# The recurrent layer's preparation rewritten: k-tile hand-over of blends and projections, padded tokens, packed key roots, decays beside the first projection

## The chip, the cores and the metric

One core of one Trainium2 chip. The metric is the device time of one execution in microseconds (us). In the profile PE is TensorE (matmul) and PEld its weight load, DVE is VectorE, ACT ScalarE, POOL GpSimd and SP SyncE.

## The reference

Two blocks follow one another: first two hybrid layers (sparse attention, gated linear attention, pooling, a convolved feed-forward), then four layers with a gating mixer, a recurrent mixer, a latent attention and again a gating mixer. Only the features of the recurrent mixer are touched. It runs over 768 tokens: 256 of context and 512 of the sequence, which are two separate sequences. In fp32, with 16 heads of 64:

```
h    = rms_norm(x) * (1 + scale) + shift
xx   = 0.5 * (previous token + next token) - h      # zero beyond either end of each sequence
xs_c = h + xx * mu_c                                # six blends, c = 0..5
r, k, v, z = xs_0 @ W_0, xs_1 @ W_1, xs_2 @ W_2, xs_3 @ W_3      # 1024 x 1024 each
w_n  = w0_n + tanh(xs_4 @ L1_n) @ L2_n              # decays, n = two directions, rank 64
a_n  = sigmoid(a0_n + (xs_5 @ A1_n) @ A2_n)
kk   = (k * k_k) / sqrt(sum over the head of (k * k_k)^2 + 1e-12)
k_n  = k * (1 + (a_n - 1) * k_a)
bonus sums: sum over the head of r * r_k * (k_0 + k_1), times v
```

The scan that follows reads r, kk, k_n, kk * a_n, v and the decays of both directions; the output reads z and the bonus.

## The kernel before

Activations lie with the 1024 channels on partitions, as 8 tiles (k when they are read, m when they are written), and the tokens in the free dimension, in two segments of 256 and 512 (`segs`). Weights come in slabs of 2048 columns (1 MB) into a ring of 4 slots; SyncE issues the loads in a fixed order, and each waits until the slab four places earlier is used up. The order here is rw_l1 0, rw_l1 1, rw_l2, then four slabs each of rw_in for r, k, v and z; a slab holds two tiles m. PSUM has 8 banks, each taken in turn from a ring by `take` and freed by the instruction that reads it last. Each engine has its own program, written out by hand and in order; semaphores are the only links. Four functions write the stage: `features_pe_`, `features_act`, `features_dve`, `features_pool`.

The stage goes as follows. Squares for the norm are summed beside the layer before. `roots_dve`, `roots_act` and `spread_pe` (L478) make and spread the inverse roots, `normed_dve` (L490) scales all 16 pieces, `modulated_act` (L1504) shifts them. When all are there, VectorE makes xx in seven instructions (L1901 to L1905), then a blend of eight instructions into the one buffer `xs` (`lerp_dve`, L1889). TensorE multiplies blend 4 by the first low-rank weights, in four products (two directions, two segments, 64 columns wide); then VectorE writes blend 5 into the same buffer, and so on in the order 4, 5, 0, 1, 2, 3. TensorE waits for the last tile of a blend, and VectorE for the last product of the blend before:

```
    lerp_dve(pl, e, 4)
    e.wait_ge(*S_.lora_made.at(4, 1, 256))
    lerp_dve(pl, e, 5)
```

After the low rank come 24 products for the decays (L330), whose sigmoids (L1801) go to memory through two stages, then r: 8 tiles of 16 products (L518), copied by VectorE (L1921) and stored.

For k, the work of a tile lies beside the next tile's projection, behind its first segment: in `derive` TensorE makes four products of the rates a (L1734) and sums the squares of the scaled keys over the head with the table blk64 (L360), ScalarE copies k (L1838), takes the sigmoids (L1815), one square (L378) and the square root (L382), VectorE scales the keys (L1934), squares one segment (L396), adds the epsilon (L401), takes the reciprocal over all 768 columns on all partitions (L404, 1.75 us for 256 columns and 3.35 for 512), normalizes (L1936), mixes (L1941) and multiplies (L1944). GpSimd multiplies the two k_n (L1998) and issues five stores a tile. The keys, the rates and k_n have one buffer each, so ScalarE waits for the stores of one tile before it writes the rates of the next. The sums for the bonus (L1744) come two tiles later. v has transposes (L336) behind its second segment, which wait for ScalarE's copy of the same tile (L1857). z has only the projection (L1868).

Of the kernel before, what the change touches and what calls it, by code (L numbers as in the profile page):

```python
# [9 lines left out]
ALU = mybir.AluOpType  # L10
# [184 lines left out]
DMA_SIGNALS = ("const", "cols", "x_in", "pos", "sgu_w", "sgu_b", "res", "a2", "lw0", "lw1", "r_out", "kk_out",  # L195
# [271 lines left out]
def spread_pe(pl, e, key, segs):  # L467

    S_ = pl.S
    e.wait_ge(*S_.inverse_roots.at(key))  # L470
    for seg in segs:
        o, n = quarters(segs, seg)
        at = ("rs", key, seg[0])
        ps = take(pl, at)
# [1185 lines left out]

def lay_features(pl):
    A, b = Arena(pl), Place()
    b.segs = list(NSEG)
    b.h, b.xx, b.xs = A(8, N), A(8, N), A(8, N)
    b.hk = lambda k, s: b.h[:, k, s[0]:s[0] + s[1]]
    b.tw, b.ta, b.a2 = A(2, N), A(2, N), A(2048)
    b.sq = [A(512), A(512)]
    at = A.at
    b.stage = [A(1024) for _ in range(2)]
    A = Arena(pl, at)  # L1670
    b.kr, b.kb, b.an, b.kd = A(2, N), A(N), A(2, N), A(2, N)
    b.rs, b.omk, b.cfs = A(N), A(8), A(2, N)
    A = Arena(pl, at)
    b.vv, b.bo, b.vt = A(2, N), A(2, N), A(2, N)
    A = Arena(pl, at)
    b.zz = A(2, N)
    b.x = lambda k, s: b.xs[:, k, s[0]:s[0] + s[1]]
    return b


LERPS = (4, 5, 0, 1, 2, 3)
# [11 lines left out]

def features_pe_(pl, e):
    S_, b = pl.S, pl.feat
    segs = b.segs
    spread_pe(pl, e, ("mod", 1), BOTH)
    for c in (4, 5):
        key = ("rw_l1", c - 4)
        w = slab(pl, key, 1024, 8)  # L1700
        e.wait_ge(*landed(pl, key))
        e.wait_ge(*S_.lerped.at(c))
        for n in range(2):
            for seg in segs:
                at = ("lora", c, n, seg[0])
                ps = take(pl, at)[0:64, 0:seg[1]]
                e.wait_ge(*free(pl, at))
                product(e, ps, [(w[:, k, 64 * n:64 * n + 64], b.x(k, seg)) for k in range(8)]).then_inc(
                    *S_.lora_made.next((c, n, seg[0]), slab=key if n == 1 and seg is segs[-1] else None))
    key = "rw_l2"  # L1710
    l2 = pl.W[:, pl.slot_of[key], 0:2048]
    e.wait_ge(*landed(pl, key))
    e.wait_ge(*S_.lora_act.at(4))
    e.wait_ge(*S_.shifted.at("ones"))
    for n in range(2):
        for a in range(6):
            for hf in range(2):
                at, o = ("decay", n, a, hf), 1024 * n + 512 * hf
                ps = take(pl, at)
                e.wait_ge(*free(pl, at))  # L1720
                product(e, ps[:, :], [(b.tw[0:65, n, P * a:P * a + P], l2[0:65, o:o + 512])]).then_inc(
                    *S_.lora_made.next((n, a, hf), slab=key if (n, a, hf) == (1, 5, 1) else None))
    features_pe(pl, e, "rw_r", [("rw_in", 0, c) for c in range(4)], 8, 256, b.x, segs, [S_.lerped.at(0)])

    def derive(m):
        for n in range(2):
            for sg in segs:
                at, o = ("iclr", m, n, sg[0]), 1024 * n + P * m
                ps = take(pl, at)[:, 0:sg[1]]
                if m == 0 and n == 0:  # L1730
                    e.wait_ge(*S_.a2.at("in"))
                    e.wait_ge(*S_.lora_act.at(5))
                e.wait_ge(*free(pl, at))
                e.matmul(ps, b.a2[0:64, o:o + P], b.ta[0:64, n, sg[0]:sg[0] + sg[1]], start=True,  # L1734
                         stop=True).then_inc(*S_.iclr_out.next((m, n, sg[0])))
        rms_pe(pl, e, ("kk", m), [rows_of(b.kb)], segs, b.sq, table(pl, "blk64"))

    def bonus(m):
        for sg in segs:
            at = ("bonus", m, sg[0])  # L1740
            ps = take(pl, at)[:, 0:sg[1]]
            e.wait_ge(*S_.bonus_in.at(m))
            e.wait_ge(*free(pl, at))
            e.matmul(ps, table(pl, "blk64"), b.cfs[:, m % 2, sg[0]:sg[0] + sg[1]], start=True, stop=True).then_inc(  # L1744
                *S_.bonus_sums.next((m, sg[0])))

    def behind_k(m, seg):
        if seg[0] == 0 and m > 1:
            bonus(m - 2)
        if seg[0] == 0 and m > 0:  # L1750
            derive(m - 1)

    features_pe(pl, e, "rw_k", [("rw_in", 1, c) for c in range(4)], 8, 256, b.x, segs, [S_.lerped.at(1)],
                beside=behind_k)
    derive(7)
    bonus(6)
    bonus(7)

    def behind_v(m, seg):
        if seg[0] == 0:  # L1760
            return
        y = b.vv[:, m % 2, :]
        e.wait_ge(*S_.act_projected.at("rw_v", m, segs[-1][0]))
        for sg in segs:
            at = ("v_t", m, sg[0])
            ps = take(pl, at)
            e.wait_ge(*free(pl, at))
            for a in range(sg[1] // P):
                t = turned(pl, e, ps[:, P * a:P * a + P], y[:, sg[0] + P * a:sg[0] + P * a + P])
            t.then_inc(*S_.value_turned.next((m, sg[0])))  # L1770

    features_pe(pl, e, "rw_v", [("rw_in", 2, c) for c in range(4)], 8, 256, b.x, segs, [S_.lerped.at(2)],
                beside=behind_v)
    features_pe(pl, e, "rw_z", [("rw_in", 3, c) for c in range(4)], 8, 256, b.x, segs, [S_.lerped.at(3)])
# [3 lines left out]
def features_act(pl, e):  # L1778
    S_, b = pl.S, pl.feat
    segs = b.segs  # L1780
    modulated_act(pl, e, 1, b.hk, BOTH, lambda k, seg: [S_.residual_added.at(("sgu_o", 0), k, seg[0])])
    e.dma_start(b.a2[0:64, :], pl.ins["rw_l2"][1][0:64, :]).then_inc(*S_.a2.next("in"))
    for c, dst in ((4, b.tw), (5, b.ta)):
        for n in range(2):
            for seg in segs:
                at = ("lora", c, n, seg[0])
                e.wait_ge(*S_.lora_made.at(c, n, seg[0]))
                e.activation(dst[0:64, n, seg[0]:seg[0] + seg[1]], bank(pl, at)[0:64, 0:seg[1]],
                             ACT.Tanh if c == 4 else ACT.Copy).then_inc(
                    *S_.lora_act.next(c, frees=at) if n == 1 and seg is segs[-1] else S_.lora_act.next(frees=at))  # L1790
    u = 0
    for n in range(2):
        for a in range(6):
            for hf in range(2):
                at = ("decay", n, a, hf)
                e.wait_ge(*S_.lora_made.at(n, a, hf))
                if u == 0 and hf == 0:
                    e.wait_ge(*S_.modulated.at(1))
                if u >= 2:
                    e.wait_ge(*(S_.lw1 if u % 2 else S_.lw0).at(u - 2))  # L1800
# [1836 lines left out]
```

## Time and profile before

| | us |
|---|---|
| runs before (3) | 5655.90, 5662.35, 5680.89; median 5662.35 |
| profiled execution, its own time | 5677.09 |
| its span | 5675.3 |
| TensorE busy | 5066.3 (89%) |
| VectorE, ScalarE, GpSimd busy | 1594.8, 1054.0, 416.5 |
| mean granted clock of TensorE | 0.92 of full speed |
| the changed stage, 2647.0 to 3294.3 | 647.3 |

The times below are from the start of the span. A matmul of fp32 data is two records in the trace, each with a weight load. A row of the timeline merges like instructions that follow one another and names the form of the first; in brackets stands how long the engine was idle before it and what released it. The granted clock is a share of 2.4 GHz.

### The profile page before, as it was taken

To read this page: it belongs to the slowest core of one execution; us is meant where nothing else is said; L and a number is where in the kernel's file an instruction comes from. 1 tells how busy PE (TensorE), PEld (TensorE's weight loads), DVE (VectorE), ACT (ScalarE), POOL (GpSimd) and SP (SyncE) were. 2 spreads that over 40 slices of the span, in tenths; PEclk is the share of its full clock that TensorE was granted. 3 is DMA by queue.
4 is the path that set the end of the run, shared out by engine and by line. 5 is a ranking of instruction groups with operands and counts; after the bars stand their busy time and mean duration, and the time that the engine had idled before them with its cause. 6 is when DMAs were issued, how large, how long until landed. Compare 5 with 4: busy or idle time off the path is not lost. (4 is left out here: it accounts for less than half of the span.)

```text
span 5675.3 us, 62648 instructions
## 1 busy us (share of the span) xinstructions
PE 5066.3 (89%) x27214; PEld 2803.4 (49%) x27214; DVE 1594.8 (28%) x2792; ACT 1054.0 (19%) x2044; POOL 416.5 (7%) x331
## 2 busy tenths in 40 slices
PE   7879999978999999997976968887589999989999
PEld 3444444444444446654433557777344455554444
DVE  1261110144111101002144145655520244430000
ACT  1121000022100111101122023333111233321210
POOL 1110000010000000000022011111000010100000
PEclk9869999977999999998987988888789999989999
DMA  3222222122121111111322222111111100001221
GB/s 114 89 105 74 82 68 83 60 104 104 67 82 66 61 59 52 52 45 56 108 72 85 80 79 63 50 49 45 77 56 51 41 23 25 29 30 67 82 74 59
DMA packets 91567, 378.27 MB, mean 67 GB/s; under 512 B 7904, under 2 KB 33504, under 8 KB 61792
## 3 DMA queue, kind: packets, MB, share of 16 engines
q1 hardware_dynamic: 74688, 318.00, 16.3%
q0 software_dynamic: 9808, 37.75, 2.0%
q10 hardware_dynamic: 6800, 18.52, 0.9%
q8 instruction: 217, 3.56, 0.3%
q14 instruction: 54, 0.44, 0.0%
HBM read 334.40 MB, written 39.85 MB: 66 GB/s over the span
## 5 line engine op out<-in xcount | busy, mean ns | idle before, releaser
L518 PE MATMUL ps<-A,W 128*128 128x512 f32 (+1 forms) x6496 | 2546.9, 553 | 48.6 <-DVE A L1889 21.3
L518 PEld LDWEIGHTS ps<-A,W 128*128 128x128 f32 x6496 | 1248.1, 193 | 1307.5 <-issue 1213.6
L330 PE MATMUL ps<-A 64*64 64x64 f32 (+3 forms) x8416 | 522.0, 243 | 89.8 <-ACT A L3180 23.2
L330 PEld LDWEIGHTS ps<-A 64*64 64x64 f32 (+2 forms) x8416 | 479.9, 153 | 203.5 <-issue 124.8
L330 PE MATMUL ps<-A,W 128*128 128x512 f32 (+5 forms) x1728 | 454.7, 431 | 48.9 <-issue 39.1
L539 PE MATMUL ps<-W,A 128*128 128x512 f32 (+1 forms) x896 | 365.6, 571 | 1.8 <-ACT A L1504 1.8
L330 PEld LDWEIGHTS ps<-A,W 128*128 128x128 f32 (+2 forms) x1728 | 226.0, 165 | 260.1 <-issue 242.0
L539 PEld LDWEIGHTS ps<-W,A 128*128 128x128 f32 x896 | 173.1, 194 | 192.6 <-issue 186.9
L432 ACT ACTIVATE A<-R 128x512 f32<-128x512 f32 (+1 forms) x96 | 52.6, 574 | 805.2 <-DVE R L1514 376.5
L1634 DVE SCALAR_TENSOR_TENSOR A<-ps,V,A 128x512 f32<-128x512 f32 (+1 forms) x48 | 31.0, 661 | 486.9 <-PE ps L330 486.3
L1514 DVE SCALAR_TENSOR_TENSOR R<-ps,MOD,R 128x512 f32<-128x512 f32 (+1 forms) x48 | 31.8, 662 | 461.8 <-PE ps L518 449.7
L360 PE MATMUL ps<-A,C 128*128 128x256 f32 (+1 forms) x64 | 48.7, 861 | 126.2 <-ACT A L378 63.5
L330 PE MATMUL ps<-W,A 64*64 64x64 f32 (+4 forms) x1904 | 157.7, 263 | 3.5 <-ACT A L2389 2.8
L1650 POOL TENSOR_TENSOR A<-A 128x1536 f32<-128x1536 f32 (+1 forms) x16 | 46.4, 2901 | 1533.5 <-ACT A L1607 1533.5
L336 PE MATMUL ps<-C,A 128*128 128x128 f32 x608 | 105.3, 300 | 49.6 <-DVE A L1184 44.0
L330 PEld LDWEIGHTS ps<-W,A 64*64 64x64 f32 (+2 forms) x1904 | 128.0, 160 | 37.5 <-issue 31.9
L2159 PE MATMUL ps<-C,A 128*128 128x256 f32 x192 | 69.2, 524 | 82.4 <-DVE A L2596 66.6
L3171 ACT ACTIVATE A<-ps,A 128x256 f32<-128x256 f32 (+1 forms) x128 | 84.8, 668 | 302.7 <-DVE A L3292 302.7
L336 PEld LDWEIGHTS ps<-C,A 128*128 128x128 f32 x608 | 72.4, 149 | 135.0 <-DVE A L1184 62.2
L1448 DVE TENSOR_TENSOR A<-A,ps 128x512 f32<-128x512 f32 x44 | 30.3, 689 | 334.1 <-PE ps L518 334.1
L1607 ACT ACTIVATE A<-ps 128x256 f32<-128x256 f32 (+1 forms) x96 | 50.3, 526 | 369.9 <-PE ps L518 369.7
L3290 DVE TENSOR_REDUCE A<-ps 128x1 f32<-128x256 f32 (+1 forms) x128 | 71.4, 558 | 142.6 <-PE ps L2955 142.1
(328 smaller groups left out, 4268.4 us busy)
## 6 DMA issues: line engine op xcount, KB each, us to landing
W<-in_ada SPq DMA_DIRECT2D x48, 1024.0 KB, 5.2
W<-in_w_up SPq DMA_DIRECT2D x44, 1024.0 KB, 4.8
W<-in_w_down SPq DMA_DIRECT2D x32, 704.0 KB, 4.0
W<-in_w_in SPq DMA_DIRECT2D x18, 1024.0 KB, 4.9
W<-in_sgu_v SPq DMA_DIRECT2D x16, 1024.0 KB, 4.9
W<-in_sgu_u SPq DMA_DIRECT2D x16, 1024.0 KB, 4.9
W<-in_sgu_z SPq DMA_DIRECT2D x16, 1024.0 KB, 4.9
W<-in_sgu_o SPq DMA_DIRECT2D x16, 1024.0 KB, 4.8
```

What stands on the lines that cost most here:

```text
L330: r = e.matmul(out, a, b, start=start and i == 0, stop=stop and i == len(pairs) - 1, skip_group_check=loose)
L336: return e.transpose(out, in_, table(pl, "ident")[0:k, 0:k])
L360: e.matmul(ps, ones[0:k, :], y, start=i == 0, stop=i == len(xs) - 1).then_inc(*S.squares_summed.next((key, n), (key, "of", seg[0])) if i = ...
L432: e.activation(pl.sq[k % 2][:, cols], pl.R[:, k, cols], ACT.Square).then_inc(*S_.act_squares.next((key, k, seg[0])))
L518: t = e.matmul(ps, w[:, k, c:c + mc], x(k, seg), start=k == 0, stop=k == kt - 1)
L539: mm = e.matmul(ps, x(k0 + k, tile), w[:, k, :], start=k0 + k == 0, stop=k0 + k == kt - 1)
L1514: e.scalar_tensor_tensor(out=r, in0=bank(pl, at)[:, 0:seg[1]], scalar=modulation(pl, i, 2, m, seg), in1=r, op0=ALU.mult, op1=ALU.add).then ...
L1607: e.activation(dst[:, m, o:o + seg[1]], bank(pl, at)[:, 0:seg[1]], func).then_inc(*signal.next((i, g), frees=at) if m == 1 and seg is segs ...
L1650: e.tensor_tensor(b.uu, b.uu, b.zz, ALU.mult).then_inc(*S_.sgu_gated.next((i, g)))
L2159: t = e.matmul(ps[:, 256 * i:256 * i + 256], b.LW[:, P * (2 * j + i):P * (2 * j + i) + P], table(pl, f"tri{n}"), start=True, stop=True)
L3171: e.activation(b.pr[:, z, lo:hi], bank(pl, at)[:, 0:hi - lo], ACT.Exp, bias=m[:, 2:3], scale=b.rq[:, p % 2, 2 * i + j:2 * i + j + 1], accu ...
L3290: e.tensor_reduce(m[:, part:part + 1], bank(pl, at)[:, 0:w], AX, ALU.max).then_inc(*made.next())
```

## The change

The four functions are written anew; the rest of the kernel calls them as before.

- Tokens are padded. h, xx and xs have 771 columns, with a zero column at either end and one between the segments, so that the neighbours of all 769 inner columns are one add.
- The first blends go by k tile. VectorE scales tile k (both segments), then adds the neighbours of tile k-1 and finishes the blends 4 and 5 of it; blend 5 has a buffer of its own, `x2`. ScalarE has shifted the tile and written h * (1 - mu) for both; a blend is then that plus 0.5 * mu times the sum of neighbours. TensorE multiplies each k tile as it comes, into six banks. The second low-rank product has both directions in one product of 128 columns (the weights a2 lie on 128 rows).
- Blend 0 is made in the same way while ScalarE sees each k tile of blend 4 used. The others (1, 2, 3) are made from xx as before, but each k tile is written as soon as the last tile m = 7 of the projection before has read it; that tile and the first, m = 0, run with k outside and both segments inside.
- The decays are no longer a part of their own: four products stand behind each of r's tiles 0 to 5.
- Banks: projections take 6, 7, 0, 1, the rest 2, 3, 4, 5.
- Key roots are packed: the squares of 4 groups of 192 tokens are summed into 4 x 32 partitions (`sums`), so root and reciprocal work on 192 columns, and `spread` brings them back to all rows, by halves. VectorE's one instruction then scales by k_k and the root from PSUM; ScalarE's square takes k_k as its scale over all 768 columns.
- Keys and rates have two buffers with stores of their own; the k_n keep one. Rates stand behind the tile's own second segment, sums and spread one tile later. Transposes of v come one tile later. The bonus product is written in place.

The core of the diff:

```diff
+def wave_pe(pl, e, c, name, ready, beside):
+    S_, b = pl.S, pl.feat
+    for m in range(8):
+        key = ("rw_in", c, m // 2)
...
+        e.wait_ge(*landed(pl, key))
+        if m in (0, 7):
...
+            for k in range(8):
+                if m == 0:
+                    e.wait_ge(*ready(k))
+                for y, s in zip(ps, b.segs):
+                    t = e.matmul(y, w[:, k, :], b.x(k, s), start=k == 0, stop=k == 7)
...
 def features_pe_(pl, e):
+    for k in range(8):
+        e.wait_ge(*S_.lerped.at(4, k))
+        for n in range(2):
+            for i, s in enumerate(segs):
+                t = e.matmul(ps[2 * n + i][0:64, 0:s[1]], w[0][:, k, 64 * n:64 * n + 64], b.x(k, s), start=k == 0,
+                             stop=k == 7)
...
+        e.wait_ge(*S_.lerped.at(5, k))
+        for i, s in enumerate(segs):
+            t = e.matmul(ps[4 + i][:, 0:s[1]], w[1][:, k, :], b.y(k, s), start=k == 0, stop=k == 7)
...
+                e.matmul(ps[:, :], b.tw[0:65, n, P * a:P * a + P], l2[0:65, o:o + 512], start=True, stop=True).then_inc(
+                    *S_.lora_made.next(at, slab=key if (u, hf) == (11, 1) else None))
+
+    wave_pe(pl, e, 0, "rw_r", lambda k: S_.lerped.at(0, k), decay)
...
+    def sums(m):
...
+        for c in range(4):
+            t = e.matmul(ps[32 * c:32 * c + 32, 0:192], table(pl, "blk64", 48, 80),
+                         pl.sq[m % 2][:, 192 * c:192 * c + 192], start=True, stop=True)
...
+    def spread(m):
+        for j in range(2):
...
+            e.wait_ge(*S_.inverse_roots.at("kk", m))
+            e.wait_ge(*free(pl, at))
+            for c in range(2):
+                for i, half in enumerate(HALF):
...
+                    t = e.matmul(ps[half, 192 * c:192 * c + 192], row, pl.root[:, 0:192], start=True, stop=True)
...
+    def behind_k(m, lo):
+        if not lo:
+            if m:
+                sums(m - 1)
+            if m > 1:
+                bonus(m - 2)
             return
+        rates(m)
+        if m:
+            spread(m - 1)
...
 def features_dve(pl, e):
+    for k in range(9):
...
+            e.tensor_tensor(b.xx[:, j, INNER], b.h[:, j, 0:N + 1], b.h[:, j, 2:N + 3], ALU.add).then_inc(
+                *S_.shifted.next())
+            e.wait_ge(*S_.shifted.last())
+            part(b.xs, 4, j)
+            part(b.x2, 5, j)
...
+    for m in range(9):
+        if m:
+            root(m - 1)
+            coefficients(m - 1)
+            if m == 7:
+                for k in range(8):
+                    lerp(2, k, "rw_k")
+            normed(m - 1)
+        if m < 8:
+            mixed(m)
```

## Rows read from the trace of the kernel before

**Rows 1.** Windows view, the changed stage: us; each engine's busy time (instructions); clock; DMA.
```profile
2647.00:3294.30 647.30, 494.35 (x1409) 268.48 (x1408) 212.90 (x221) 110.23 (x188) 102.90 (x100) 0.85 0.26 85
```

**Rows 2.** Waits view of TensorE, 2640 to 3330: us in total, times, longest.
```profile
PE ps L360 <- ACT A L378: 50.9, 8, 9.4
```

**Rows 3.** Timeline of all engines, head: start us, us, engine, line, operation [idle before].
```profile
2650.18 1.35 DVE L464 RECIPROCAL A<-A 128x192 f32<-128x192 f32 x1 [0.80 <-ACT A L454]
...
2651.59 3.78 PE L478 MATMUL ps<-A,C 128*128 128x64 f32 x16 [2.64 <-DVE A L464]
...
2653.70 8.49 DVE L490 SCALAR_TENSOR_TENSOR A<-R,MOD,ps 128x256 f32<-128x256 f32 x16 [2.16 <-PE ps L478]
...
2654.27 8.67 ACT L1504 ACTIVATE A<-A,MOD 128x256 f32<-128x256 f32 x16 [4.12 <-DVE A L490]
...
2679.20 7.53 DVE L1889 SCALAR_TENSOR_TENSOR A<-A,V 128x768 f32<-128x768 f32 x8
```

**Rows 4.** Timeline of TensorE, low rank to the first k tiles.
```profile
2686.83 23.26 PE L330 MATMUL ps<-A,W 128*64 128x256 f32 x64 [31.45 <-issue]
...
2717.75 23.16 PE L330 MATMUL ps<-A,W 128*64 128x256 f32 x64 [7.67 <-issue]
...
2740.84 20.87 PE L330 MATMUL ps<-W,A 65*128 65x512 f32 x48
...
2761.54 82.72 PE L518 MATMUL ps<-A,W 128*128 128x256 f32 x256
...
2852.55 15.53 PE L518 MATMUL ps<-A,W 128*128 128x256 f32 x48 [8.29 <-DVE A L1889]
```

**Rows 5.** Timeline of TensorE, one k tile of the steady part.
```profile
2889.96 1.56 PE L1744 MATMUL ps<-A,C 128*128 128x256 f32 x4 [1.84 <-DVE A L1951]
...
2891.45 2.84 PE L1734 MATMUL ps<-A 64*128 64x256 f32 x8
...
2903.25 2.05 PE L360 MATMUL ps<-A,C 128*128 128x512 f32 x2 [8.32 <-ACT A L378]
...
2905.09 11.34 PE L518 MATMUL ps<-A,W 128*128 128x512 f32 x32
...
2919.24 1.77 PE L1744 MATMUL ps<-A,C 128*128 128x256 f32 x4 [2.81 <-DVE A L1951]
```

**Rows 6.** Timeline of TensorE, the starts of v and z.
```profile
3102.29 13.48 PE L518 MATMUL ps<-A,W 128*128 128x256 f32 x32 [4.50 <-DVE A L1889]
...
3116.46 0.88 PE L336 MATMUL ps<-C,A 128*128 128x128 f32 x6 [0.69 <-ACT A L1857]
...
3209.00 85.28 PE L518 MATMUL ps<-A,W 128*128 128x256 f32 x256 [8.48 <-DVE A L1889]
```

**Rows 7.** Timeline of ScalarE, in the same k tile.
```profile
2897.57 1.28 ACT L1815 ACT_TABLE_LOAD   x1 [5.41 <-DMA f_ka<-A]
...
2898.86 1.99 ACT L1815 ACTIVATE A<-ps,V 128x256 f32<-128x256 f32 x4
...
2902.49 0.61 ACT L378 ACTIVATE A<-A 128x512 f32<-128x512 f32 x1
```

**Rows 8.** Timeline of VectorE and GpSimd, in the k tile before.
```profile
2883.16 2.17 DVE L1941 TENSOR_SCALAR A<-A,V 128x768 f32<-128x768 f32 x1
...
2882.46 2.45 POOL L1998 TENSOR_TENSOR A<-A 128x768 f32<-128x768 f32 x1 [36.34 <-DVE A L1941]
```

**Rows 9.** Timeline of TensorE, a later stage (64-column products of two halves).
```profile
4312.31 10.57 PE L2910 MATMUL ps<-A,W 128*64 128x256 f32 x64
```

**Rows 10.** Windows view: after a long wait; one k tile.
```profile
2686.80:2691.50 4.70, 4.67 (x11) 2.59 (x12) 0.00 (x0) 0.00 (x0) 0.00 (x0) 0.50 0.01 3
...
2889.96:2919.24 29.28, 18.14 (x48) 9.43 (x49) 14.78 (x13) 8.09 (x13) 9.00 (x8) 0.83 0.24 68
```

**Rows 11.** Tile view, loads of rw_in (x16) and of rw_out (x4, together).
```profile
DMA to landing us min/median/max: 4.7/5.2/6.8
...
DMA to landing us min/median/max: 5.6/10.4/15.0
```

More of the change, by code:

```diff
@@ L1710, in features_pe_ @@
[L1710 to L1736, printed above, removed]
+    segs, side = b.segs, "2345"
@@ L1738, in bonus @@
     def bonus(m):
-        for sg in segs:
-            at = ("bonus", m, sg[0])
-            ps = take(pl, at)[:, 0:sg[1]]
+        for s in segs:
+            at = ("bonus", m, s[0])
+            ps = take(pl, at, side)[:, 0:s[1]]
             e.wait_ge(*S_.bonus_in.at(m))
             e.wait_ge(*free(pl, at))
[L1744 to L1760, printed above, removed]
-            return
+            e.matmul(ps, table(pl, "blk64"), b.cfs[:, m % 2, s[0]:s[0] + s[1]], start=True, stop=True).then_inc(
+                *S_.bonus_sums.next((m, s[0])))
+    def behind_k(m, lo):
[4 more added lines that the diff above has]
+                bonus(m - 2)
+            return
+        rates(m)
+        if m:
+            spread(m - 1)
@@ L1791, in features_act @@
-    u = 0
-    for n in range(2):
[L1793 to L1800, printed above, removed]
-                e.activation(b.stage[u % 2][:, 512 * hf:512 * hf + 512], bank(pl, at)[:, :], ACT.Sigmoid).then_inc(
-                    *S_.decay_act.next((u, hf), frees=at))
-            u += 1
@@ new lines, in features_act, with root @@
+    for u in range(12):
+        if u >= 2:
+            e.wait_ge(*(S_.lw1 if u % 2 else S_.lw0).at(u - 2))
+        for hf in range(2):
+            at = ("decay", u, hf)
+            e.wait_ge(*S_.lora_made.at(at))
+            e.activation(b.stage[u % 2][:, 512 * hf:512 * hf + 512], bank(pl, at)[:, :], ACT.Sigmoid).then_inc(
+                *S_.decay_act.next((u, hf), frees=at))
+    def root(m):
+        x = pl.root[:, 0:192]
+        e.wait_ge(*S_.mean_squares.at("kk", m))
+        e.activation(x, x, ACT.Sqrt).then_inc(*S_.roots.next(("kk", m)))
@@ L1844, in features_act @@
-    derive(7)
-    bonus(6)
-    bonus(7)
+            if m >= 2 and s is segs[0]:
+                e.wait_ge(*S_.value_turned.at(m - 2, segs[1][0]))
+                e.wait_ge(*S_.bonus_made.at(m - 2))
+            e.activation(b.vv[:, m % 2, s[0]:s[0] + s[1]], bank(pl, at)[:, 0:s[1]], ACT.Copy).then_inc(
+                *S_.act_projected.next(at, frees=at))
+            if s is segs[0] and m == 0:
+                root(7)
+            if s is segs[0] and m < 2:
+                bonus(6 + m)
@@ L1908, in features_dve @@
+    for k in range(8):
+        part(b.xs, 0, k)
     e.memset(b.tw[64:65, :, :], 0.0).then_inc(*S_.shifted.next())
```

492 lines of the change are left out of this document (299 added, 193 removed).

## The prediction

> **What bounds the kernel now.** The profiled execution took 5677.1 us (span 5675.3), 14.7 above the median of the runs, 5662.35. The change touches one stage. The windows view cuts it out, from the last matmul of the gating layer (2647.0) to the last z matmul (3294.3) [rows 1]: 647.3 us with TensorE busy for 494.4 at a mean granted clock of 0.85. No other engine is busy for more than a third, so the stage is bound by TensorE and by what TensorE waits for. The waits view names the largest cause: eight waits of matmuls for the squares of the key norms [rows 2]. The timelines then give six stretches, whose bounds are starts of matmuls:
> - head, 2647.0 to 2686.8: 39.8 us, TensorE nearly idle while VectorE and ScalarE make h, its shift and the first blend [rows 3, 4]
> - low rank, to 2740.8: 54.0, two projections of 23.2 with a blend's wait of 7.7 between them [rows 4]
> - decays and r, to 2844.3: 20.7 and 82.7, dense [rows 4]
> - k, to 3102.3: 258.0, with 8.3 of blend wait ahead [rows 4], then a period of 29.3 a tile; 2889.96 to 2919.24 is one, and the others have this form [rows 5]
> - v, to 3209.0: 106.7, 11.9 a tile and a blend wait of 8.5 [rows 6]
> - z, to 3294.3: 85.3 [rows 6].
>
> They sum to 647.3.
>
> **The change, part by part.** *Head.* The spread roots are complete at 2651.6 + 3.8 = 2655.4; VectorE now waits for both segments, 1.7 later than before. Its 16 normed pieces take 8.5, so 1.06 a k tile, and a blend over 768 columns 0.94 (8 in 7.53) [rows 3]. Per k tile it now does 1.06, an add and two blends: 1.06 + 3 x 0.95 + 0.15 for dependent starts (my estimate) = 4.1. ScalarE has 1.1 of shifting [rows 3] and two scalings of some 0.9 (0.61 for 512 columns [rows 7]) = 2.9, hidden behind 4.1; if VectorE were free, 2.9 would be the pace. POOL's three memsets and the constants that VectorE makes lie under the squares and roots; without that cover they would cost under 1. The first blend is ready after two norms, an add and a blend: 2655.5 + 4.2 = 2659.7. Head 12.7, saved 27.1.
>
> *Low rank.* Projection 4 has the same matmuls; projection 5 has both directions in one 128-column product, half as many. At full rate 768 columns over 8 k take 10.3 (82.7 for eight tiles [rows 4]); so 20.6 + 10.3 = 31, 3.9 a k. VectorE brings a k each 4.1, so it sets the pace and TensorE, 95% busy, ends behind it: 2655.5 + 8 x (1.06 + 2.95) = 2687.6, last products 2689.4. The first 4.7 us after a long wait run at 0.50, the low level of 1.2 GHz [rows 10]; the 2.3 lost are caught up in the slack. 29.7 against 54.0, saved 24.3.
>
> *Decays beside r.* The same products, 20.7 + 82.7 = 103.4 [rows 4]. The blend for r costs VectorE 7.5 from 2687.6 and TensorE takes 1.3 a k for the first tile, so it is not late; the row of ones and the tanh end near 2698, ahead of the first decay at 2699.6. But the weight ring has four slots, and the fourth r slab goes into that of the second-stage decay weights. Until now that was free before r began; now the last decay, at the end of tile 5, frees it and tile 6 needs it at once. SP stands at that load, and the first three k slabs are issued right behind it. Bounds: such a load landed in 4.7 at best; of four issued together the first landed in 5.6, the last in 15.0 [rows 11]. I take 5.6 + 0.3 for the signal, since ours is the first of four. After the 8.3 wait at 2852.55 the next 48 matmul records took 15.5, where dense ones take 13.8 (1.33 tiles of 10.3) [rows 4]: 1.7 more. Stall 7.6. 111.0 against 103.5, lost 7.5. The sigmoids' waits for stores were off the path and stay so.
>
> *k.* Off the path go the roots over 768 columns on all rows, the extra scaling pass, the single buffers that held ScalarE for a store [rows 7], and the blend's wait at the start (r's last tile hands k tiles back one by one, each blend 0.95, each use 1.3). TensorE per tile: rates 2.84, bonus 1.6, projection 10.3 [rows 4, 5]; packed sums, four column groups of 192, some 0.5; two spreads, together 768 columns in pairs of halves. Halves run together: line 2910 has 12288 columns in 64 records, twice the 6144 of a full-width tile, in 10.6 [rows 9], the time of one tile. So the spreads are 1.3; were they apart, 2.6. One wait stays: the spreads need banks that the rates' sigmoids free. After the tile's last product ScalarE has copy 0.6, square 0.85, table load and the first sigmoids [rows 7]: 0.1 + 0.6 + 0.05 + 0.85 + 1.29 + 0.45 = 3.35, and 3.85 for the second. TensorE has done its 2.84 and waits 0.5 to 1. Tile period: 4.9 (rates, wait, spreads) + 10.3 + 0.5 + 1.6 + 0.2 = 17.5. The others must fit: ScalarE 7.8 (copies 2.0, square 0.85, loads 2.6, root 0.4, sigmoids 2.0); VectorE 9 to 12 (root 0.4 + 1.35 for 192 columns [rows 3], coefficients 2.0, norms 1.1, products 1.9, mixes 1.3 to 4); POOL two multiplies of 2.45 [rows 8] and five stores, 9.2. All fit, and each link of the chain (sums at 8.5 after the tile, root by 12, spread at 17.5 + 3.4) has 5 us to spare. First tile 10.3, second 13.7, five of 17.5, last 4.9 + 10.3: 126.7. Late next: VectorE's blends for v stand behind root 6, whose sums TensorE makes only after tile 7. Root at 4.0, coefficients 6.0, first blend 7.0; TensorE's spread of tile 6 waits for sigmoids and is over at 8.0. So v starts at 134.7. Against 258.0, saved 123.3.
>
> The Trainium skill (ScalarE: Activation LUTs, What ACT_TABLE_LOAD costs) gives a switch of sets 1283 ns plus a drain of about 1380. The trace shows only the first: the load at 2897.57 is followed by its activation at 2898.86 [rows 7], so the measurement decides. By the page the wait for the banks would be 1.4 longer in each of eight tiles, an estimate of 11 us more.
>
> *v.* Eight tiles 82.6; turns 0.9 each [rows 6], now a tile later and so without their 0.7 wait, 6.2; sums, bonuses and spread of tile 7, 4.9; 2.0 of wait for root 7 (VectorE does the eight blends first); 2.1 for z's first blend, behind turn 6: 97.8, saved 8.9. *z.* 82.6 and one turn: 83.5, saved 1.8; its last store is where it was, so the scan starts as before. Four gaps of 1 to 3 us remain. After one of 2.8 the group in [rows 5] came late and the next was slow, and 3 to 5 us at half rate lose about 2; I add 3 in all (0 to 6).
>
> Sum: 27.1 + 24.3 - 7.5 + 123.3 + 8.9 + 1.8 - 3 = 174.9. The profiled execution would take 5502; against the median, 5487.
>
> Later stages are not edited, but they enter the shared ring of banks at another turn: price 0, bounded by 3 either way, since each such bank has whole tiles of slack.
>
> **Rivals.** (1) *The k loop is paced by another engine.* For: a scaling of VectorE took 2.17 while POOL multiplied [rows 8], and all work in a tighter ring of banks. Against: busy times of 8 to 12 under 17.5. A period of 22 gives 6 x 4.5 = 27 more: 5514. (2) *The clock stays low in the low-rank stretch.* For: a k tile with TensorE 62% busy had a clock of 0.83 [rows 10]. Against: 95% busy here. At half rate 31 us of products are 62: 32 more, 5519. (3) *A switch of tables costs twice its row*, 1.3 in each of eight tiles: 5497. (4) *Slower: stores hold the k loop.* For: before, ScalarE waited 5.4 for a store in each tile [rows 7]. If the single kd buffers hold the next rates, nothing overlaps: TensorE 14.6, square, root, spread, norms, mixes, multiplies and coefficients 18, stores 4.2, and a landing of 6.8 to 15.0 [rows 11] give 43.6 to 51.8 a tile. It loses from 17.5 + 175/7 = 42.5 on and gives 5670 to 5727. Against: only VectorE's mix waits for that store, and it landed half a tile earlier. (5) *The fourth slab lands with the last of its burst*, 15.0: 10 more, 5497.
>
> **How the numbers follow.** Own sum 0.60, rival 1 0.14, rival 2 0.06, rival 3 0.05, rival 4 0.02, rival 5 0.10, and 0.03 for a part that gains nothing (the head and low rank, or half of k: about 5545). Own bounds: landing -1, gaps -3, later stages -3, pace -2 and the scatter of runs 8 make 5470; upward alike, 5505. The range takes in rivals 1, 2, 3 and 5: 5470 to 5524. A measurement of this kernel tells about 0.5% (28 us) from no change; only rival 4 is not beyond it: faster 0.97, same 0.01, slower 0.02.
>
> **What would show it.** Right: the first low-rank matmul some 13 us after the gating layer's last; its products in groups each 4.1; a gap of 5 to 7 between r's tiles 5 and 6, ended by a landing; k starts without a gap, 17.5 a tile; gaps of about 2 before v's second tile and before z; the stage 472 us, clock above 0.95. Wrong: a period over 20 with VectorE or POOL named, a low-rank stretch at 0.5, a slab gap over 9, or a scan that starts late.

## The result and the profile after

The changed kernel takes 5491.86 us (median of 4 runs, 5480.95 to 5501.22) against 5666.45 (4 runs, 5655.9 to 5680.89): a ratio of 0.969, 95% interval 0.9659 to 0.972, 174.6 us less. Forecast were 5487 and a range of 5470 to 5524. In a later comparison of five rounds the ratio was 0.9699 (0.9671 to 0.9727).

The head of the page of the changed kernel; the profiled execution took 5480.95 us:

```profile
span 5479.2 us, 62884 instructions
...
PE 4986.2 (91%) x27342; PEld 2765.4 (50%) x27342; DVE 1544.5 (28%) x2779; ACT 1070.9 (20%) x2058; POOL 406.8 (7%) x334
```

The windows view over the changed stage, which answers to [rows 1], whole and by the six stretches of the prediction (us; busy time of TensorE, its weight loads, VectorE, ScalarE, GpSimd, with instructions; granted clock; DMA share; GB/s):

```profile
2636.80:3111.60 474.80, 442.34 (x1537) 248.44 (x1536) 163.09 (x208) 126.95 (x201) 93.12 (x103) 0.97 0.34 116
...
2636.80:2648.55 11.75, 3.45 (x34) 2.76 (x33) 7.05 (x13) 5.84 (x9) 1.29 (x4) 0.74 0.89 350
2648.55:2684.24 35.69, 35.69 (x97) 14.30 (x97) 33.66 (x42) 27.14 (x36) 0.00 (x0) 0.94 0.06 20
2684.24:2795.10 110.86, 105.08 (x306) 58.64 (x305) 24.90 (x32) 18.92 (x32) 12.32 (x19) 0.97 0.38 138
2795.10:2932.26 137.16, 122.18 (x512) 68.56 (x511) 57.84 (x72) 56.01 (x89) 53.98 (x47) 0.98 0.43 134
2932.26:3028.08 95.82, 92.43 (x332) 55.29 (x331) 31.28 (x43) 12.29 (x23) 20.27 (x24) 1.00 0.38 123
3028.08:3111.60 83.52, 83.50 (x262) 48.90 (x262) 8.36 (x10) 6.75 (x14) 5.26 (x10) 1.00 0.15 57
```

The stage takes 474.8 us instead of 647.3. TensorE works 442 of them instead of 494 and idles 32 instead of 153. Most of the gain, 120 us, is idle time removed; the other 52 are work done in less time, since the clock is at full speed more often (0.97 instead of 0.85) and some products are fewer or overlap.

| stretch | before | forecast | after |
|---|---|---|---|
| head | 39.8 | 12.7 | 11.8 |
| low rank | 54.0 | 29.7 | 35.7 |
| decays and r | 103.5 | 111.0 | 110.9 |
| k | 258.0 | 134.7 | 137.2 |
| v | 106.7 | 97.8 | 95.8 |
| z | 85.3 | 83.5 | 83.5 |
| half rate after gaps | in the rows | 3 | in the rows |
| stage | 647.3 | 472.4 | 474.8 |

The two profiled spans differ by 196.1 us, 23.6 more than the stage. That part stands in code that the change does not touch: the time ahead of the stage is 2636.8 instead of 2647.0, behind it 2367.6 instead of 2381.0. Over the profiled executions shown here the first lay between 2618 and 2647, the second between 2367.6 and 2394.8, whatever was edited. So a single total says little about an edit worth 10 us, and the experiments are read by their stage.

The waits of TensorE from 2640 to 3150, largest first, which answer to [rows 2] (total, times, longest; left out are two of the scan behind the stage and two shorter ones of 1.6 and 1.0):

```profile
PE ps L1811 <- ACT A L1926: 13.9, 7, 2.0
...
PE ps L331 <- DMA W<-in_rw_in: 5.8, 1, 5.8
...
PE ps L1749 <- DVE A L2009: 4.4, 1, 4.4
PE ps L479 <- DVE A L465: 2.6, 1, 2.6
PE ps L1718 <- DVE A L2044: 1.8, 1, 1.8
```

The eight waits for squares, 50.9 us, are gone. New are seven for the banks that the sigmoids free (L1926), six of 2.04 and one of 1.68, and one of 5.8 for a weight slab. The timeline of TensorE shows them in place: the low rank, the late slab, and one k tile, which answers to [rows 5].

```profile
2648.55 4.85 PE L1749 MATMUL ps<-A,W 128*64 128x256 f32 x8 [4.40 <-DVE A L2009]
2653.33 1.56 PE L1754 MATMUL ps<-A,W 128*128 128x256 f32 x4
2654.82 2.79 PE L1749 MATMUL ps<-A,W 128*64 128x256 f32 x8
2657.55 1.56 PE L1754 MATMUL ps<-A,W 128*128 128x256 f32 x4
2659.03 2.80 PE L1749 MATMUL ps<-A,W 128*64 128x256 f32 x8
...
2763.38 3.60 PE L1772 MATMUL ps<-W,A 65*128 65x512 f32 x8
2772.76 12.00 PE L331 MATMUL ps<-A,W 128*128 128x256 f32 x32 [5.78 <-DMA W<-in_rw_in]
...
2818.02 1.56 PE L1788 MATMUL ps<-A 64*128 64x256 f32 x8
2821.62 1.52 PE L1811 MATMUL ps<-A,C 128*64 128x192 f32 x16 [2.04 <-ACT A L1926]
2823.08 3.72 PE L331 MATMUL ps<-A,W 128*128 128x256 f32 x16
2826.73 0.53 PE L1797 MATMUL ps<-A,C 128*32 128x192 f32 x8
2827.19 1.56 PE L1820 MATMUL ps<-A,C 128*128 128x256 f32 x4
2828.59 7.03 PE L331 MATMUL ps<-A,W 128*128 128x512 f32 x16
2835.55 1.56 PE L1788 MATMUL ps<-A 64*128 64x256 f32 x8
```

From 2818.02 to 2835.55 are 17.5 us, where a tile took 29.3. In the low rank a k tile takes 4.21 (from 2654.82 to 2659.03) without any wait on VectorE: TensorE itself sets the pace there (experiment 4, in which every blend is ready before TensorE starts, has the same 4.21). VectorE would be faster, 3.9 from one k tile to the next (2649.25 to 2653.16):

```profile
2649.25 1.14 DVE L2018 SCALAR_TENSOR_TENSOR A<-R,MOD,ps 128x256 f32<-128x256 f32 x2
...
2653.16 1.13 DVE L2018 SCALAR_TENSOR_TENSOR A<-R,MOD,ps 128x256 f32<-128x256 f32 x2
```

What ScalarE does in that k tile:

```profile
2818.13 0.60 ACT L1945 ACTIVATE A<-ps 128x512 f32<-128x512 f32 x1 [5.47 <-PE ps L331]
2818.76 0.94 ACT L1957 ACTIVATE A<-A,V 128x768 f32<-128x768 f32 x1
2819.71 1.28 ACT L1926 ACT_TABLE_LOAD   x1
2821.01 1.99 ACT L1926 ACTIVATE A<-ps,V 128x256 f32<-128x256 f32 x4
```

The first sigmoid starts 1.30 us after the load of its table. The wait for stores that stood ahead of this load before, 5.4 us in [rows 7], is gone.

### The profile page after: what moved, and what is told of

Read it like the earlier page. It is cut to its first block and busy times, and to the rows that moved or that the text cites. A ratio compares the mean times of both kernels' runs of the same rounds, so it can differ in the third digit from the quotient of the medians.

```text
span 5479.2 us, 62884 instructions
## 1 busy us (share of the span) xinstructions
PE 4986.2 (91%) x27342; PEld 2765.4 (50%) x27342; DVE 1544.5 (28%) x2779; ACT 1070.9 (20%) x2058; POOL 406.8 (7%) x334
## 5 line engine op out<-in xcount | busy, mean ns | idle before, releaser
L519 PE MATMUL ps<-A,W 128*128 128x512 f32 (+1 forms) x5472 | 2193.5, 561 | 27.2 <-POOL A L2938 8.8
L519 PEld LDWEIGHTS ps<-A,W 128*128 128x128 f32 x5472 | 1043.2, 192 | 1135.6 <-issue 1081.1
L331 PE MATMUL ps<-A,W 128*128 128x512 f32 (+3 forms) x2368 | 662.6, 444 | 15.5 <-DMA W<-in_rw_in 5.8
L331 PEld LDWEIGHTS ps<-A,W 128*128 128x128 f32 (+2 forms) x2368 | 351.0, 174 | 304.9 <-issue 273.0
L331 PE MATMUL ps<-W,A 64*64 64x64 f32 (+3 forms) x1856 | 137.7, 255 | 3.9 <-ACT A L2548 2.8
L331 PEld LDWEIGHTS ps<-W,A 64*64 64x64 f32 (+1 forms) x1856 | 119.6, 160 | 26.3 <-issue 21.6
L2741 DVE TENSOR_TENSOR A<-ps,C 64x512 f32<-64x512 f32 x96 | 66.1, 689 | 124.2 <-PE ps L331 121.9
```

The source lines that it names most:

```text
L331: r = e.matmul(out, a, b, start=start and i == 0, stop=stop and i == len(pairs) - 1, skip_group_check=loose)
L519: t = e.matmul(ps, w[:, k, c:c + mc], x(k, seg), start=k == 0, stop=k == kt - 1)
L2741: e.tensor_tensor(dst[HALF[c], 8 * g:8 * g + 8, :], by_heads(bank(pl, at)[HALF[c], :]), masked_by(pl, mask, HALF[c], 8), ALU.mult).then_in ...
```

## The experiments

Each edits the changed kernel. "Stage" is always the stretch of the table above; the changed kernel has 474.8 (478.3 in the second profiled execution of it). The 3.5 between the two are groups of products at half rate behind the same gaps: 13.59 instead of 12.00 behind the late slab, and one k tile more. Experiments 1 to 10 are one execution each, so a difference of the stage under some 4 us shows nothing by itself; the single rows do.

**1. Three decay units behind each of r's tiles 0 to 3.** The slot of the fourth r slab comes free two tiles earlier.

```diff
-        if not (lo and m < 6):
+        if not (lo and m < 4):
...
-        for u in (2 * m, 2 * m + 1):
+        for u in range(3 * m, 3 * m + 3):
```

> Three decay units stand behind each of r's tiles 0 to 3 instead of two behind tiles 0 to 5, so that the slot of the decay weights is free two tiles before the fourth r slab is used. Theory (the slot is late, not the load slow): the gap of 5.8 us before r's tile 6 and the slow tile behind it (12.0 instead of 10.5) go, and the stage takes 474.8 - 7.3 = 467.5 us. Rival (the sigmoids wait for their stores, which a burst of three units makes worse): TensorE waits for banks inside the bursts instead, and the stage stays at 472 to 477.

Measured: stage 465.8 us, total 5473.71. Where the wait stood, r's products are now one row of 96 records:

```profile
2731.94 31.14 PE L331 MATMUL ps<-A,W 128*128 128x256 f32 x96
```

9.0 us gained: 5.8 of gap, 1.5 of half rate behind it (12.00 instead of 10.49), and some 1.6 because fewer of the later groups ran slowly. The cause of the slab's gap is shown: it was the place of the last decay.

**2. All decays as a part of their own, ahead of r**, as before the change.

```diff
-    wave_pe(pl, e, 0, "rw_r", lambda k: S_.lerped.at(0, k), decay)
+    for m in range(6):
+        decay(m, 1)
+    wave_pe(pl, e, 0, "rw_r", lambda k: S_.lerped.at(0, k), lambda m, lo: None)
```

> All 24 decay products stand ahead of r again, the rest is the changed kernel. Theory (the decays cost TensorE 20.7 us wherever they stand; beside r they only cover the wait for the tanh, and in exchange hold a slab slot): the slab gap goes (7.3), but TensorE now waits some 9 us after the low rank for tanh and the row of ones and starts at half rate (2): stage 476 to 480, against 474.8. Rival (their place is worth what they take): 20 us more, 495.

Measured: stage 492.7, total 5500.45. The slab's gap was gone, yet the stage was 17.9 longer. TensorE's timeline and the windows view of this kernel:

```profile
2669.66 41.30 PE L1772 MATMUL ps<-W,A 65*128 65x512 f32 x48 [3.49 <-DVE A L2036]
```

```profile
2669.66:2690.00 20.34, 20.34 (x24) 8.11 (x25) 6.83 (x8) 7.54 (x12) 2.69 (x5) 0.50 0.43 169
2690.00:2710.90 20.90, 20.90 (x26) 8.11 (x25) 0.00 (x0) 7.16 (x12) 3.20 (x6) 0.50 0.39 157
2710.90:2716.00 5.10, 5.10 (x15) 2.91 (x14) 0.00 (x0) 0.60 (x1) 0.53 (x1) 0.79 0.75 215
```

The same 48 records took 20.87 before the change [rows 4]. Here they began behind a gap of 3.5 us and ran from the first to the last at 1.2 GHz, without any gap in between, until r's products of 128 rows followed and the clock rose. I had expected the full clock within a few us. The 17.9 are, within 0.2, 20.4 for the slow block, 3.5 for the gap (some 9 were expected) and 1.1 for r's slow first tile (11.63 instead of 10.50), less the 7.3 of the slab; that the stage came near the rival's 495 is chance. Experiment 9 tests what was to blame.

**3. Blends handed over whole**, for r, k, v and z.

```diff
-                    e.wait_ge(*ready(k))
+                    e.wait_ge(*ready(7))
...
-        e.wait_ge(*S_.projected.at(before, "k", 7, k))
+        e.wait_ge(*S_.projected.at(before, "k", 7, 7))
```

> The four blends for r, k, v and z are handed over whole: TensorE's first tile waits for the last k tile of the blend, and VectorE starts a blend of k, v and z when the projection before has ended. Theory: the waits come back as 10 before r, 8.5 before k, 6 more before v and 6.6 more before z, 31 in all, and each leaves a half-rate start that loses 1.5 to 2: stage 506 to 514. Rival (the hand-over by k tile matters little, since VectorE had little to do at the ends): under 10 us.

Measured: stage 502.7, 27.9 more; total 5503.17. Waits view and the three starts in the timeline:

```profile
PE ps L1718 <- DVE A L2044: 21.2, 3, 8.3
```

```profile
2786.39 12.91 PE L1718 MATMUL ps<-A,W 128*128 128x256 f32 x32 [7.71 <-DVE A L2044]
...
2929.76 12.90 PE L1718 MATMUL ps<-A,W 128*128 128x256 f32 x32 [5.18 <-DVE A L2044]
...
3034.39 13.48 PE L1718 MATMUL ps<-A,W 128*128 128x256 f32 x32 [8.31 <-DVE A L2044]
```

The three waits are 21.2 us instead of 1.8, and each first tile takes 2.4 to 3.0 longer than the usual 10.5 at half rate behind its gap, together 7.8: 27.2 of the 27.9. Before r the wait was only 0.7, not the 10 expected, since the last k tile of blend 0 comes just after r could start; that is why the stage lies under the 506 to 514.

**4. The first blends handed over whole.** TensorE starts the low rank only when the last k tile of blend 5 is there.

```diff
+    e.wait_ge(*S_.lerped.at(5, 7))
     for k in range(8):
         e.wait_ge(*S_.lerped.at(4, k))
```

> TensorE waits for all eight k tiles of blends 4 and 5 before the first low-rank product; VectorE and ScalarE do the same work in the same order. Theory: the low-rank stretch (31 us of products) no longer lies beside the 27 us in which the blends are made: 24 to 27 more, stage 499 to 502; the blend for r then comes well ahead of its use. Rival (the slow clock at the start eats what the overlap gives): 10 to 15 more.

Measured: stage 502.9, 28.1 more; total 5532.34, with one wait of 31.7 for VectorE where 4.4 stood. Head and low rank gained 46.3 (93.8 to 47.5); the overlap by k tile is 28.1 of it (24 to 27 were expected). The other 18 belong, by subtraction, to what this edit leaves in place: padding, fewer instructions, the buffer of its own for blend 5 and the doubled second product; they were not tried singly. The low rank without VectorE beside it, in this run:

```profile
2685.99 2.79 PE L1750 MATMUL ps<-A,W 128*64 128x256 f32 x8
...
2690.20 2.80 PE L1750 MATMUL ps<-A,W 128*64 128x256 f32 x8
```

**5. Key roots over 768 columns on all rows**, neither packed nor spread. The sums are one product for each segment; add, root, reciprocal and scaling work on 768 columns, one tile later as in the changed kernel.

```diff
-        for c in range(4):
-            t = e.matmul(ps[32 * c:32 * c + 32, 0:192], table(pl, "blk64", 48, 80),
-                         pl.sq[m % 2][:, 192 * c:192 * c + 192], start=True, stop=True)
...
+            e.matmul(ps[:, 0:s[1]], table(pl, "blk64"), pl.sq[m % 2][:, s[0]:s[0] + s[1]], start=True,
...
-        if m:
-            spread(m - 1)
```

> The packed roots are undone: the squares are summed over the head on all 128 rows for 768 columns, and epsilon, root and reciprocal (5.1 us of VectorE) work on all of them in place in the key buffer; sums in four columns groups and spreads fall away. Order, double buffers and distances stay. Theory (the overlap has shortened the tile, not the packing): VectorE has 14 us of work a tile and fits, TensorE is free of the spreads and of the wait for their banks: 15.2 to 16 a tile against 17.5, stage 460 to 466. Rival (the short reciprocal carries it): VectorE sets the pace at 20 or more, stage 490 or more.

Measured: stage 466.3, 8.5 less; total 5502.0. A k tile in the timeline of TensorE, and the start of v:

```profile
2842.31 1.56 PE L1788 MATMUL ps<-A 64*128 64x256 f32 x8
2843.80 3.72 PE L331 MATMUL ps<-A,W 128*128 128x256 f32 x16
2847.36 1.46 PE L1797 MATMUL ps<-A,C 128*128 128x256 f32 x4
2848.66 1.45 PE L1819 MATMUL ps<-A,C 128*128 128x256 f32 x4
2849.94 7.03 PE L331 MATMUL ps<-A,W 128*128 128x512 f32 x16
2856.91 1.56 PE L1788 MATMUL ps<-A 64*128 64x256 f32 x8
...
2923.60 13.57 PE L1718 MATMUL ps<-A,W 128*128 128x256 f32 x32 [5.46 <-DVE A L2039]
```

A tile takes 14.6 instead of 17.5, with TensorE busy throughout. The reciprocal grows to 4.95 us on VectorE, but under other work. At the start of v, where the blends stand behind it, it is on the path: the handover waits 5.5 instead of being covered, and later 3.8. So packing is not what shortened the k tile: it costs 2.9 in each and saves time only at the end of k. By stretches, k took 17.7 less and v 5.9 more; head, low rank and r, which the edit does not touch, took 3.3 more in this execution, so without them it is worth nearer 12 than 8.5.

**6. The rates of both directions issued one direction after the other** (the two loops of `rates` exchanged), since they took 1.56 us instead of the 2.84 of [rows 5].

> The rates' products are issued direction by direction, so that products on the two halves of the rows no longer alternate. Theory (alternating halves overlap, which is why four took 1.56 and not 2.84, but the sigmoids set the time of the spreads): the four products take 2.84 again, the wait behind them shrinks from 2.04 to about 0.8, the tile stays at 17.5 and the stage at 474 to 476. Rival (the products are on the path): 1.3 a tile, 485. If the products still take 1.56, the alternation is not the reason.

Measured: stage 475.1, total 5505.03; the rates took 1.57 and the wait behind them stayed at 2.04. The order does not matter. What the change altered is where the operands lie: before, both directions read rows 0 to 63, now one reads rows 0 to 63 and the other 64 to 127. The single records of the trace show that the two directions now run together: they start in pairs, 0.01 us apart, in both orders of issue, where before they started 0.2 to 0.4 apart. This run has the order of issue of the kernel before and differs from it in these products by the placement, which leaves that as the likely cause; it was not tried by itself. The Trainium skill (TensorEngine Tiling (Array Packing), Theoretical Speedup) gives up to twice the speed for contractions of at most 64 rows; 2.84 to 1.56 is a factor of 1.8.

**7. Five banks for the side products, three for the projections.**

```diff
-    segs, side = b.segs, "2345"
+    segs, side = b.segs, "12345"
...
```

> Five banks (1 to 5) for the small products and three (6, 7, 0) for the projections instead of four and four. Theory (the spreads wait for banks that the rates' sigmoids free): the first spread now follows a bank freed long before and the second waits for the first sigmoid alone; the wait of 2.04 a tile falls to 1 or less, 7 to 10 us in the k wave, and the handover from r to k costs 1 to 1.5: stage 466 to 470. Rival (the spreads wait for the reciprocal or for something else of the chain): no change in the wait.

Measured: stage 471.4, 3.4 less; total 5499.81. The wait fell from 2.04 to 1.24 a tile (a period of 16.9), and the two spreads now took 0.87 each, apart, instead of 1.52 together. With three banks the projection of k waited 1.6 for VectorE's copies of r, so a part of the gain was given back. Shown are the shorter wait and period; the 3.4 of the stage are no more than the scatter, and the 466 to 470 expected were not reached.

**8. The shared ring of banks advanced by 178 behind z**, for the faster stretch behind the stage (2367.6 instead of 2381.0).

> After the last z product the shared bank ring is advanced by the 178 places that the stage took before the change, so that all later stages use the same banks as the kernel before. Theory (the bank turn has no price, and the 13 us by which the later stages were shorter in the profile of the changed kernel are scatter): the part after the stage takes 2360 to 2385 us, within the scatter of both profiles (2367.6 and 2381.0). Rival (the other turn of banks gives some 10 us): that part is at 2380 or more and stays there.

Measured: stage 476.4, total 5515.78, the part behind the stage 2394.8. By the letter this lies in the rival's range (2380 or more). But the changed kernel itself, with its own turn of the ring, had 2388.0 in its second profiled execution, and the other experiments, which leave the turn alone, 2380.6 to 2391.4; so 2367.6 was one short execution and not a gain of the turn. A price of a few us for either turn is not excluded.

**9. All decays in one block behind r's tile 0.** The same block as in 2, but behind dense products instead of behind a gap.

```diff
-        if not (lo and m < 6):
+        if not lo or m:
             return
...
-        for u in (2 * m, 2 * m + 1):
+        for u in range(12):
```

> All 24 second-stage decay products of the stage stand in one block behind r's tile 0 (before the change they stood behind a dense projection too, and took 20.87 us for 48 records at a granted clock of 1.00; put ahead of all of r, behind a gap of 3.49 us, they took 41.3 us at 0.50). Theory: only the cold start made them slow, so behind dense 128-row products they take 20.6 to 21.0 us at a clock near 1.0; the slab's gap behind tile 5 goes as well, and the stage takes 466 to 468 us against 474.8. Rival: a block of these 65-row products falls to the low level wherever it stands; then they take 30 to 41 us and the stage 477 to 487 us.

Measured: stage 471.9, total 5498.71. The block in the windows view:

```profile
2698.91:2721.70 22.79, 21.38 (x49) 8.79 (x48) 1.17 (x3) 11.07 (x20) 5.35 (x10) 1.00 0.52 208
```

22.8 us at a clock of 1.00, 1.4 of it in three waits for ScalarE's sigmoids. So the form of the product does not lower the clock: the low clock at its start made it slow in 2. The stage is 4 above its 466 to 468: 2 in this block, 1.6 in one more k tile at half rate behind its 2.0 us gap (2.83 and 4.02 where 1.52 and 3.72 are usual), and 1.0 in the head, where the spread of the roots ran at half rate (3.78 instead of 2.77).

**10. One buffer for the rates**, on the kernel of 5, where nothing else waits in the k loop. ScalarE writes the sigmoids of a tile when both stores of the tile before have landed.

```diff
-        if m >= 2:
+        if m:
             for n in range(2):
-                e.wait_ge(*kept(S_, f"ka{n}", m - 2))
+                e.wait_ge(*kept(S_, f"ka{n}", m - 1))
...
```

> The version with wide roots (stage 466.3 us, 14.6 a k tile, no wait in it), with one difference: the rates have one buffer again, so ScalarE writes the sigmoids of a tile only when both stores of the scaled rates of the tile before have landed. Theory: the second buffers are a part of the gain in k. The second of these stores is issued 4.4 us into the tile, lands 3 to 4 later, and table load and sigmoids take 3.3: they end at 11.3 to 12.5 instead of 5.0, and the sums of the next tile and the bonus product need their banks. TensorE then waits some 6 us in each of seven tiles behind its first segment (for ScalarE's sigmoids, L1921): period 20 to 21, stage 502 to 512. Rival: the lag of the sums by a tile is what shortened the tile, and the store lands under other work: period 14.6 to 15, stage 466 to 470. The whole of before's period (29.3) back would say that the buffers alone did it.

Measured: stage 504.8, 38.5 more than in 5; total 5520.25. Waits of TensorE, then one tile of ScalarE:

```profile
PE ps L1797 <- ACT A L1921: 28.0, 6, 6.1
```

```profile
2873.99 0.94 ACT L1952 ACTIVATE A<-A,V 128x768 f32<-128x768 f32 x1
2880.35 1.28 ACT L1921 ACT_TABLE_LOAD   x1 [5.43 <-DMA f_ka<-A]
2881.65 2.00 ACT L1921 ACTIVATE A<-ps,V 128x256 f32<-128x256 f32 x4
```

The 5.4 us of [rows 7] are back. The period is 20.3 in the tile shown and 18.3 to 23.6 over five tiles, 21.7 in the mean (from 2808.55 to 2917.22), which is above the 20 to 21 expected. Of the 14.7 between 29.3 (before) and 14.6 (experiment 5) the second rate buffer is thus 7.1 with this order of the work: 5.0 of wait and 2.1 of products at half rate behind it (2.90 and 2.76 where 1.45 are usual). The other 7.6 belong to what was not undone, among it: the rates' products run together, the keys have two buffers, the square stands ahead of ScalarE's wait, and the sums do not stand right behind the rates. Only the first has a price in the rows, 1.3; how much each of the others does was not tried.

**11 and 12. A version beyond the change**, beside the changed kernel in five rounds each: three decay units a tile (1), wide roots (5), and VectorE's blends for v ahead of the root and coefficients of tile 6, those for z one tile earlier.

```diff
+            if m == 7:
+                for k in range(8):
+                    lerp(2, k, "rw_k")
             root(m - 1)
             coefficients(m - 1)
...
+        if m == 6:
+            for k in range(8):
+                lerp(3, k, "rw_v")
```

> Three edits together: three decay units behind each of r's tiles 0 to 3 (no late slab), the key roots over 768 columns without packing and spreading, and VectorE's blends for k's and v's successors moved ahead of the root and coefficients of the last tiles. Theory: the gains add up: 466.3 of the stage with wide roots, less 9.4 for the slab's gap and the slow tile behind it, less about 10 of waits at the two handovers (5.46 and 3.77 with half-rate starts): stage 446 to 450 us, the whole about 25 us or 0.5% below the changed kernel, ratio to the kernel before 0.962 to 0.967. Rival: the waits only move (roots and coefficients then come late for the last tiles' mixes, and the scan's or the sigmoids' banks are held), stage 457 to 466 us and a whole within 0.3% of the changed kernel.

> The changed kernel itself, for the comparison on the same chip in as many rounds: a ratio to the kernel before of 0.966 to 0.972 again, the stage at 474 to 477 us. Were the gain partly one of the chip used the first time, the ratio would lie nearer 1 (0.975 or more) while the stage stays at 475.

Measured against the same runs of the kernel before: this version 5468.98 us (5455.6 to 5481.94), ratio 0.9646 (0.9622 to 0.9669); the changed kernel 5492.96 (5479.0 to 5516.14), ratio 0.9699 (0.9671 to 0.9727). The stages are 450.6 and 478.3, the second 1.3 above the 474 to 477 expected. It beats both kernels; the medians lie 24.0 us apart, and the intervals do not quite touch. Its waits in the stage are those of the head and these two:

```profile
PE ps L1788 <- ACT R L1930: 4.3, 1, 4.3
PE ps L1819 <- DVE A L2080: 3.8, 1, 3.8
```

The stage is 0.6 above the upper end of what was expected: v and z no longer wait for a blend, but the rates of tile 7 now wait 4.3 for ScalarE's bonus copy, where in experiment 5 they waited 1.2 and v's start another 5.5. The handover's wait moved and shrank, and the 3.8 stayed.

## Why the prediction was right

**The bound and its causes.** The stage was bound by TensorE's waits, and these went where the prediction said. It named the six stretches; five came within 2.5 us of their forecast, and the sum within 2.4 of 474.8. That closeness is in part luck: 6.0 too little for the low rank and 2.5 for k stand against 2.0 too much for v, 0.9 for the head and the 3 booked apart for half rate. The median came 4.9 above the forecast. Of the 172.5 us of the stage, experiments 3, 4 and 10 put a price on 27.9, 28.1 and 38.5 (the last with wide roots); the rest of the gain was not taken apart.

**Head.** Forecast 12.7, measured 11.8: the spread of the roots took 2.8 instead of the 3.8 of [rows 3], and from its end to the first product 4.4 passed, where 4.2 was forecast. The 1.0 is the clock and not the change: in six of the thirteen profiled executions with the new stage the spread took 3.8.

**Low rank: the mis-sized term.** Forecast 29.7, measured 35.7. The step that failed is "at full rate 768 columns over 8 k take 10.3; so 20.6 + 10.3 = 31, 3.9 a k", with VectorE's 4.1 above it. That price came from long groups of like products. Here groups of four products 64 columns wide and of two 128 wide alternate, and in the rows above the first lasts 2.73 from its start to the next (2654.82 to 2657.55) instead of 20.6 / 8 = 2.58, the second 1.48 instead of 1.29: 4.21 a k tile. It is not that each product goes to another bank, for r's tile 0 does that too and took 10.50. Nor is it VectorE, since experiment 4 has the same 4.21. What differs is the change of width, twice a k tile at some 0.17. The single records bear this out: inside a group they start 0.215 or 0.43 apart as everywhere, and the extra stands at the border and the first step behind it (0.20 into the 128-column group, 0.15 into the 64-column one). Groups of the same two products between others of 128 columns took 1.28 to 1.30 in experiment 5. The Trainium skill (TensorEngine Tiling (Array Packing), Key Properties) says that a change of tiling mode drains TensorE; the rows agree in kind, with 0.15 to 0.20 as its cost, and no run here changes the widths alone. TensorE therefore had no slack, and the 2.0 us that the first group lost at half rate (4.85 instead of 2.80) were not caught up, as the prediction had them: 8 x 4.21 + 2.0 = 35.7.

**Decays beside r.** Forecast 111.0, measured 110.9. The slab stall was forecast at 7.6 and is 5.8 + 1.5 = 7.3; in the other executions that have it, it is 7.5 to 9.3 (gaps of 6.0 to 6.3, tiles of 11.97 to 13.59), so 7.6 lies at the lower end. Experiment 1 shows its cause and gives it back. Rival 5, the slab landing last of its burst, did not come.

**k.** Forecast a period of 17.5, measured 17.5, but two terms erred against each other: the rates took 1.56 instead of 2.84, since the two directions run together on separate halves of the rows (experiment 6), and the wait behind them 2.04 instead of 0.5 to 1. The prediction gave this overlap to the spreads, and took the rates from [rows 5] although the change moves their directions to separate halves too. The end of that wait is set by ScalarE (copy, square, table load, first sigmoids), so the shorter rates only made TensorE wait longer, and the period was right by the prediction's own chain. Experiment 7 moves this wait with one more bank. The stretch took 2.5 more than forecast, in groups at half rate (5.32 instead of 3.72, 12.15 instead of 10.60), which the sum booked apart.

**v and z.** Forecast 97.8 and 83.5, measured 95.8 and 83.5. The waits forecast at 2.0 and 2.1 are 1.6 and 1.8, the seven turns took 0.66 each from start to start instead of 0.9, and v starts 7.8 behind the end of k's last tile, where 8.0 was forecast.

**The rivals.** (1) No other engine paces the k loop: VectorE is busy 8.2, ScalarE 7.6 and GpSimd 7.9 of 17.5. (2) The clock in the low rank was 0.94. (3) A switch of tables costs its row, 1.30 from load to activation. The prediction's chain without a further drain frees the banks 3.35 to 3.85 behind the tile's last product, and the spreads start 3.6 behind it (2818.02 to 2821.62). By the drain that the Trainium skill gives (ScalarE: Activation LUTs, What ACT_TABLE_LOAD costs) it would have been 1.4 later; the measurement decides. (4) No store holds the loop; experiment 10 shows what one rate buffer fewer costs, 7.1 a tile. (5) See above.

**Half rate after gaps.** Forecast 3 beside the two terms named. Measured in the rows: 5.32 for 3.72 and 12.15 for 10.60, together 3.2. The size is luck: the prediction booked it for four single gaps of 1 to 3, and the gaps of 1.05, 1.59, 1.68 and 1.80 were all followed by full rate. The loss stands behind two of the six waits of 2.04 in the k loop, which the prediction had at 0.5 to 1.

## What to carry to other kernels

Handing over by tiles is worth the whole wait and the half-rate start behind it: at three places the waits were 19.4 us and the slow starts another 7.8. When an ordered ring carries the loads, ask of each moved step which slot it keeps: the last decay, moved beside r, held back a slab and cost 7.3 us. Before making a side task small (packed roots), see whether it is on the path: here it was so only at the end of k, and its extra products and bank waits cost 2.9 in each tile.

## What the runs showed that was not expected

- A block of products with 65 rows, begun at the low clock behind a gap of 3.5 us, stayed at 1.2 GHz for its whole 41.3 us although TensorE never idled in it; behind dense products of 128 rows the same block ran at 2.4 GHz, in 20.87 and 22.8 us. The clock rose only when 128-row products followed. A tile of 128-row products behind the slab's gap of 5.8 to 6.3 us lost only 1.5 to 3.1 us before it was back at full rate. Whether rows, columns or the share of the array decide was not tried.
- A gap of 2.04 us in the k loop, the same in each tile, was followed by full rate in most tiles and by half rate in up to three of them, at different tiles from one execution to another. That is 1.6 of the 3.5 us by which two stages of the same kernel differ.
- Two products on separate halves of the rows run together in either order of issue (their records start 0.01 us apart).
- Parts of the kernel that no edit touches differ by up to 29 us ahead of the stage and 27 behind it between executions.
